# A two-block transformer in split fp32 on one core: head norms and output columns regrouped at the end of the last attention, and one weight split ahead of the residual's norm

## What is computed

```python
def gmlp_mixer(h, w_in, v_gain, w_sp, b_sp, w_out):      # the gate
    uv = jax.nn.gelu(h @ w_in)
    u, v = jnp.split(uv, 2, axis=-1)
    v = layer_norm_gain(v, v_gain)
    ...
    z = jnp.einsum('gts,bcsgd->bctgd', w_sp * causal, v)
    z = z + b_sp.T[None, None, :, :, None]
    return (u * z.reshape(B, S, D_GATE)) @ w_out

def diff_attention(h, k, v, w_q, lam_vecs, subln, w_o, lambda_init):   # the last attention
    ...
        p = jax.nn.softmax(s, axis=-1)
        a = p[:, :, 0] - lam * p[:, :, 1]
        return jnp.einsum('bhts,bhsd->bhtd', a, vf)
    ...
    o = rms_norm_2(o, subln) * (1.0 - lambda_init)       # per head of 128 channels
    return o.reshape(B, S, V_WIDTH) @ w_o
```

## Time and profile before

| | |
|---|---|
| median of the runs | 1892.91 us (1891.71 to 1892.91, 3 runs) |
| the profiled execution | 1893.12 us, of which the span is 1891.3 us |
| busy: PE / PEld / DVE / ACT / POOL | 98% / 81% / 58% / 41% / 14% |
| granted TensorE clock, mean of the span | 0.991 |
| DMA | 174.48 MB, 92 GB/s on average |

### The profile page before, as it was taken

How to read it: one execution, slowest core, us unless ns; L and a number is a source line. 1 busy time by engine, 2 the same in 40 slices (tenths; PEclk the granted TensorE clock), 3 DMA queues, 4 the chain that set the end, 5 groups by cost and what they waited for, 6 DMA issues and landing times.

```text
span 1891.3 us, 24875 instructions
## 1 busy us (share of the span) xinstructions
PE 1861.0 (98%) x8756; PEld 1524.8 (81%) x8756; DVE 1097.0 (58%) x1575; ACT 768.1 (41%) x1181; POOL 257.8 (14%) x206
## 2 busy tenths in 40 slices
PE   7999999999999999999999999999999999999998
PEld 6877888788888888887888888888787888888886
DVE  5867976777677624676544442254888654444323
ACT  4226664355545413563422322143557433323212
POOL 4702320020000001301100000021643110000001
PEclk9999999999999999999999999999998999999998
DMA  4232332122222332222223223332111223222232
GB/s 174 96 105 74 101 101 78 56 90 92 96 100 89 122 100 89 91 88 89 89 100 100 89 100 100 99 100 97 66 62 34 67 91 99 99 94 96 99 100 78
DMA packets 62837, 174.48 MB, mean 92 GB/s; under 512 B 5428, under 2 KB 23988, under 8 KB 62648
## 3 DMA queue, kind: packets, MB, share of 16 engines
q1 hardware_dynamic: 61424, 169.50, 27.1%
q10 hardware_dynamic: 1016, 2.92, 0.5%
q0 software_dynamic: 336, 1.25, 0.2%
HBM read 171.54 MB, written 2.10 MB: 92 GB/s over the span
## 4 chain that ended last, share of the span: by engine, by line
PE 90%; DVE 5%; ACT 1%; issue 1%; POOL 1%; DMA 1%; SPq 0%; POOLq 0%; DVEq 0%; ACTq 0%
PE ps L472 29%; PE ps L474 28%; PE ps L473 28%; PE ps L999 1%; DVE w_lo L1670 1%; POOL square_sum L2448 1%; DMA w_raw<-in_weights 1%; PE ps L1010 1%; ACT w_hi L1108 0%; PE ps L954 0%; DVE at_e L1898 0%; PE ps L492 0%; DVE sg_z L2195 0%; DVE sg_t L2191 0%; PE ps L667 0%
## 5 line engine op out<-in xcount | busy, mean ns | idle before, releaser
L1670 DVE TENSOR_TENSOR w_lo<-w_raw,w_hi 128x1024 fp32r<-128x1024 f32 x315 | 405.5, 1288 | 461.5 <-ACT w_hi L1108 461.1
L472 PE MATMUL ps<-xg_hi,w_hi 128*128 128x512 f32 (+1 forms) x1448 | 566.0, 391 | 11.5 <-DVE w_lo L1670 10.0
L473 PE MATMUL ps<-xg_lo,w_hi 128*128 128x512 f32 (+1 forms) x1448 | 559.0, 386 | 0.0
L474 PE MATMUL ps<-xg_hi,w_lo 128*128 128x512 f32 (+1 forms) x1448 | 558.6, 386 | 0.0
L1108 ACT ACTIVATE w_hi<-w_raw 128x1024 fp32r<-128x1024 f32 x315 | 331.6, 1053 | 540.1 <-PE ps L474 534.6
L472 PEld LDWEIGHTS ps<-xg_hi,w_hi 128*128 128x128 f32 x1448 | 273.7, 189 | 76.9 <-DVE w_lo L1670 16.7
L474 PEld LDWEIGHTS ps<-xg_hi,w_lo 128*128 128x128 f32 x1448 | 273.6, 189 | 54.9
L473 PEld LDWEIGHTS ps<-xg_lo,w_hi 128*128 128x128 f32 x1448 | 273.9, 189 | 53.5 <-issue 1.0
L472 PE MATMUL ps<-hid_hi,w_hi 128*128 (+1 forms) x528 | 205.5, 389 | 0.0
L474 PE MATMUL ps<-hid_hi,w_lo 128*128 (+1 forms) x528 | 205.4, 389 | 0.0
L473 PE MATMUL ps<-hid_lo,w_hi 128*128 (+1 forms) x528 | 205.4, 389 | 0.0
(11 more groups left out here) (368 smaller groups left out, 2445.9 us busy)
## 6 DMA issues: line engine op xcount, KB each, us to landing
w_raw<-in_weights SPq DMA_DIRECT2D x315, 512.0 KB, 3.3
out_cols<-result SPq DMA_DIRECT2D x8, 256.0 KB, 2.2
x<-in_x_cols SPq DMA_DIRECT2D x2, 512.0 KB, 5.8
x<-in_x_cols SPq DMA_DIRECT2D x1, 1024.0 KB, 9.0
squares<-in_mem_cols ACTq DMA_DIRECT2D x1, 512.0 KB, 3.8
sp_w<-in_spatial ACTq DMA_DIRECT2D x1, 512.0 KB, 4.3
sp_b<-in_spatial_bias ACTq DMA_DIRECT2D x1, 512.0 KB, 5.1
dil<-in_dil_table POOLq DMA_DIRECT2D x1, 448.0 KB, 9.2
```

The source lines that it names most:

```text
L472: nc.tensor.matmul(to, wh, xh, start=start, stop=False)
L473: nc.tensor.matmul(to, wh, xl, start=False, stop=False)
L474: return nc.tensor.matmul(to, wl, xh, start=False, stop=stop)
L1670: nc.vector.tensor_tensor(w_lo[:, u % 2, :], w_raw[:, u % 2, :], w_hi[:, u % 2, :].bitcast(F32), ALU.subtract).then_inc(w_ready, 1)
```

## The change

It has two parts that don't meet.

**At the gate**, DVE's split of the third unit of `a_out` moves from behind the eight instructions on x to ahead of them; `into_residual` gets `done = 1` and leaves that split out.

**At the end of the last attention**, heads 0 and 1 are spread in step 26 into banks 2 and 3, heads 2 and 3 in step 27 into banks 7 and 2. DVE multiplies heads 0 and 1 in step 26, now ahead of its split, heads 2 and 3 in step 27; ACT and DVE round and subtract heads 0 and 1 in step 27, heads 2 and 3 in step 28. As bank 2 also takes the sums, those of head 4 move from step 28 to step 29, and the later sums wait until four heads are multiplied. The first four columns move from steps 30, 31, 33, 35 to 29, 30, 31, 33, and with them their additions and the two splits behind them (steps 31 and 34 in place of 32 and 36).

```diff
-        COLUMN_ITEMS = (BO_EARLY, BO_EARLY + 1, BO_EARLY + 3, BO_EARLY + 5)
+        COLUMN_ITEMS = (BO_EARLY - 1, BO_EARLY, BO_EARLY + 1, BO_EARLY + 3)
+        LATER_SUMS = (29, 32, 36)
...
                 if j == 0:
                     pe.wait_ge(a3["out_lo"], 4)
-                if j < 2:
-                    pe.wait_ge(a3["normed"], 3 + j)
-                else:
+                if j >= 2:
                     pe.wait_ge(early["added"], ADDED["bo_early"] + j - 1)
...
-                if n >= 12 and n % TB == 0 and n // TB - 3 < N_DIFF - 1:
+                if n >= 12 and n % TB == 0 and n // TB - 3 < 4:
                     head_sums(n // TB - 3)
...
                 if n == 26:
+                    head_spread(0, 2)
+                    head_spread(1, 3)
+                if n == 27:
                     pe.wait_ge(kv["qk"], 2 * N_DIFF)
-                    head_spread(0, 7)
-                if n == 27:
-                    head_spread(1, 3)
+                    head_spread(2, 7)
                     pe.wait_ge(a3["normed"], 1)
-                    head_spread(2, 7)
-                if n == 28:
-                    pe.wait_ge(a3["normed"], 2)
-                    head_spread(3, 3)
+                    head_spread(3, 2)
+                if n in LATER_SUMS:
+                    pe.wait_ge(a3["normed"], 4)
+                    head_sums(4 + LATER_SUMS.index(n))
...
+            split(FIRST["a_out"] + 2)
             for c in range(KC):
                 nc.vector.scalar_tensor_tensor(out=x[:, c, :], in0=x[:, c, :], scalar=column("g_first", c), in1=first["r"][:],
                                                op0=ALU.mult, op1=ALU.mult).then_inc(x_ready, 1)
             dve.wait_ge(x_ready, KC * NORM["a"])
-            into_residual("a_out", KC, "ffn0", "ffn_norm0", 0)
+            into_residual("a_out", KC, "ffn0", "ffn_norm0", 0, 1)
...
+                if n == 26:
+                    head_normed(0, 2)
+                    head_normed(1, 3)
                 if panel_due(n):
                     split(qk0 + EARLY_PANELS - 1 + n // 2 + 2)
...
-                if n == 26:
-                    head_normed(0, 7)
                 if n == 27:
-                    head_normed(1, 3)
                     head_normed(2, 7)
+                    head_normed(3, 2)
                     head_lo(0)
+                    head_lo(1)
                 if n == 28:
-                    head_normed(3, 3)
-                    head_lo(1)
                     head_lo(2)
-                if n == 29:
                     head_lo(3)
```

More of the change, by code:

```diff
@@ L1613, in diff_item @@
                     head_hi(0)
+                    head_hi(1)
                 if n == 28:
-                    head_hi(1)
                     head_hi(2)
-                if n == 29:
                     head_hi(3)
@@ L1704, in into_residual @@
                 elif n > LAST:
-                    split(u0 + 2)
+                    if not done:
+                        split(u0 + 2)
                     split(u0 + 3)
```

## The result

| kernel | median us | range of 15 runs | profiled execution | its span | mean granted clock |
|---|---|---|---|---|---|
| before | 1893.04 | 1891.71 to 1894.75 | 1893.12 | 1891.3 | 0.991 |
| changed | 1896.41 | 1893.56 to 1896.85 | 1895.94 | 1894.1 | 0.992 |

The ratio is 1.0017, with a 95% interval of 1.0010 to 1.0024. The changed kernel is 3.4 us slower, which is inside the 0.2% that the prediction calls the same. The forecast was 1894.8 us, so the direction is right and 1.6 us are missing. The time lies at the upper edge of the forecast's own case.

What follows compares the result with a forecast made beforehand. PE was taken as the bound, so only its waits and clock could move the time. -1.74 (gate) + 1.8 (steps 26 to 30) + 1.8 (steps 34 to 37) = +1.9 us, giving 1894.8 us, range 1890.5 to 1898.3 us.

Steps and rivals of the forecast that it cites:

- the forecast's own case: Whole kernel: a time of 1893 to 1896.7 us, given a chance of 0.44.
- The gate, -1.74 us: Third unit of `a_out`: PE's wait for DVE's split goes, 1.74 us gained, bounds 1.5 to 1.74 us.
- Steps 26 to 30, +1.8 us: Last attention: PE waits for `probs`, still owes head 4's sums, and the low clock ends later; 1.8 us lost.
- T: Time at which the full clock returns after the attention's low stretch, forecast between 1457.2 and 1460.4.
- the prediction's formula: Delay in steps 26 to 30: 2.1 + (T - 1456.2) - (T - 1451.2) / 2 + 0.87 us.
- Steps 34 to 37, +1.8 us: Attention's tail: without column 3 as cover, PE waits for squares and last subtraction; 1.8 us lost, bounds +0.7 to +2.1.
- X: End of `weigh` in step 33, 1470.47 before the change; the tail's times are counted from it.
- the two waits that the prediction named: Ahead of step 37's `weigh`: PE waits 1.2 us on ACT's `da_v` and 0.5 us on DVE's `at_pt_lo`.
- the slower rival: Steps 35 to 37: idle time drops the clock for 3.4 us, costing 1.7 us; up to 1897.6 us, chance 0.22.
- The clock stays up: Last attention: head 1's spread fills the wait, PE keeps full clock, -2.0 for +1.8; 1891.0 us, chance 0.12.
- Only the gate: The attention's end comes out even and only the gate's gain remains; 1891.2 us, chance 0.17.
- both gain: Both ends gain: the clock stays up and the tail has no wait; 1889.2 us, chance 0.05 (or more gain).

Runs made afterwards that it cites:

- gate_only: Kernel before with the gate's part of the change alone; 1890.93 us, ratio 0.9989.
- gate_again: Second timing of the kernel before with the gate's part alone; 1891.26 us, ratio 0.9991.
- heads_only: Changed kernel without the gate's part, so the attention's part alone against the kernel before; 1897.76 us, ratio 1.0028.
- split_late: Changed kernel with ACT's and DVE's second split back in step 36 instead of 34; 1894.03 us, ratio 1.0004.
- tail_fill: Changed kernel plus five unread matmuls of 512 columns ahead of head 6's sums in step 36; 1893.57 us, ratio 1.0003.
- sums28_cols_old: Changed kernel with the four columns back in steps 30, 31, 33, 35 and head 4's sums back in step 28; 1890.21 us, ratio 0.9983.
- sums28_again: Second timing of the changed kernel with old column places and head 4's sums in step 28; 1890.28 us, ratio 0.9985.
- gate_fill: Kernel before with the gate's part plus 7, 4 and 6 unread matmuls ahead of the turns of steps 27, 28, 29; 1891.21 us, ratio 0.9992.
- col3_late: Changed kernel with column 3 back in step 35 and its split behind it; 1892.81 us, ratio 1.0003.

## Why the prediction was right, and where its sizes were off

**The gate, -1.74 us: right.** The trace shows -1.73 at the unit and -1.79 at step 27; *gate_only* and *gate_again* gave -1.95 and -1.81. DVE's idle time ahead of the split was 0.78 us against 0.85, and PE has no wait for the fourth unit.

**Steps 26 to 30, +1.8 us: right in each step.** DVE's split took 1.21 us without POOL beside it, forecast 1.2 in place of 2.29. Step 29's turn started at 1451.21 in before's time, forecast 1451.2, and column 0 at 1452.71 + 1.79 = 1454.50, forecast 1454.55. The clock came back at 1456.1 + 1.8 = 1457.9, near the early end of 1457.2 to 1460.4. For that T the prediction's formula gives 2.1 + 1.7 - 3.35 + 0.87 = 1.3 us, and one wait of 0.3 us that it didn't know, ahead of a turn at 1468.86, makes 1.6; the marks show 1.70. Three other profiles with the same work here (*heads_only*, *split_late*, *tail_fill*) had a low stretch of 17 us in place of 13.6, so the late end of the range for T was real too. PE's new idle time was 2.98 us and not 2.1, because PE reached the place sooner; that changes nothing, since the turn starts when `probs` is written. This idle time is nevertheless where the design loses: *sums28_cols_old* shows that it holds the 1.9 us of head 4's sums, which the change had moved out of it.

**Steps 34 to 37, +1.8 us: the wait was right, its price was not.** Squares at X + 2.6 (forecast X + 2.7), last subtraction at X + 4.1 (X + 3.9 to X + 4.1), last `weigh` at X + 4.13 (X + 4.0), a loss of 1.92 us. *split_late* confirms the split as 1.16 us of it, with X + 2.97. Of the two waits that the prediction named, 1.2 us on `da_v` was 0.96 us, and that of 0.5 us on `at_pt_lo` was covered by the stretched sums. Up to this mark the whole sum was +1.83 against a forecast of +1.9.

**The step that was off** is that the sum took the tail at the full clock. The low clock stood in it only as the slower rival, with a chance of 0.22 and a price of 1.7 us, one stretch of 3.4 us. Its mechanism was true: the clock was at 0.50 from 1476.7 to 1483.4 in the changed kernel and for as long in *heads_only*, and *tail_fill* took just that away and left the starts of the tail ahead of it in place. The stretch was twice as long as priced and cost 2.8 us. I had argued against it from the gate, where PE paused for about as long and the clock stayed; but there large matmuls stood on both sides, and here the 3.2 us between 1474.18 and 1477.36 held 0.9 us of them, then idle time and one-column sums. The fall at 1490.4 behind the 4-row spreads looks like the nearer precedent. In the tail, though, the idle time was needed: the trace of *split_late* has the same one-column sums behind the same `weigh`, but not the 0.96 us of idle time ahead of them, and its clock stayed at 1.00 there.

**What hid the miss.** The profiled execution stayed inside the forecast's case because it did not have the fall behind the spreads of heads 4 to 7, worth 1.62 us. So +1.83 up to the last `weigh`, +2.82, -1.62 and -0.2 in the rest of the kernel make the +2.8 of the spans. The medians differ by 3.4, because the profiled execution was 0.5 us faster than the median of the changed kernel. One execution of its 15 took 1893.56 us, with a mean granted clock of 0.993; the others took 1895.82 to 1896.85 us, with 0.990 to 0.992. That would fit a tail without the low stretch, but no trace of it exists. Whether the missing fall belongs to the change stays open. Of two profiles of one and the same kernel, *sums28_cols_old* had a low stretch of 3.4 us there and *sums28_again* had none, and their medians are 0.07 us apart. It is not decided by the order of the work alone. That the time came out inside the forecast's case is thus luck in part.

**The other rivals.** *The clock stays up* fell: the first low stretch was as long in the changed kernel (13.5 us in its row) as before (13.6 us). Head 1's spread, 4-row matmuls inside the wait, did not hold it, and the trace of *gate_fill* shows that matmuls of 128 rows in the same waits can, for ten microseconds. *Only the gate* and *both gain* fell with the two waits. By the Trainium skill ("TensorE: Matmul & The Clock Gate", "Why this matters for your kernels") idle gaps of TensorE are what loses the clock. The tail agrees in direction, since *tail_fill* closed the one idle gap there and kept the clock, but that gap was 0.96 us, shorter than the gaps that this section warns of; the fall at 1490.4 with PE busy throughout does not agree.

Open is also why the clock falls earlier or later in programs that are equal up to that place: the first block's stretch at 166 was at 0.50 for 6.8 us in the profile of before, for 3.4 in *gate_only* and not at all in the changed kernel, with no edit near it. It cost nothing there: ACT's rounding at the gate starts at 862.63 before and at 862.64 in the changed kernel.

## What to carry to other kernels

When work is moved out from between a producer and its consumer, ask what it covered. Then price the idle time that appears twice: once by its length, and once by the clock that may fall behind it. The second price was the larger one here (2.8 us behind 1.9). Small work with no urgent consumer, such as the one-column sums, belongs in a wait that exists anyway: there it was worth its whole 1.9 us.

## What I had not expected of the hardware

Five matmuls whose result nobody reads, 1.2 us of PE's time, made the kernel 2.8 us faster. In the changed kernel the low clock came 1.65 us after the end of the last `weigh` matmul ahead of the wait (1474.78 + 0.27) and stayed for 6.7 us, although PE was busy for 6.63 of them, from 1477.36 on with matmuls of 128 rows and 128 to 512 columns. A wait of 1.07 us in step 33 of *col3_late* and one of 1.96 us between starts at the gate, both with such matmuls close on each side, left the clock at 1.00. And with fillers in the waits of steps 27 to 29 the same program took from 1888.4 to 1894.5 us, a wider range than any other kernel's here.
